# The closing LayerNorm of a fused decoder step: moments on ScalarE, gain and shift in three-operand steps on VectorE

## The reference, cut to what matters

```
def layer_norm(x, g, b):
    xf = x.astype(jnp.float32)
    mu = jnp.mean(xf, -1, keepdims=True)
    var = jnp.mean(jnp.square(xf - mu), -1, keepdims=True)
    y = (xf - mu) * lax.rsqrt(var + LN_EPS) * g.astype(jnp.float32) + b.astype(jnp.float32)
    return y.astype(x.dtype)
...
        f = moe_ffn(h, P['w_router'], P['router_bias'], P['ex_wg'][l], P['ex_wu'][l], P['ex_wd'][l])
        h = layer_norm(ALPHA * h + f, P['ln3_g'][l], P['ln3_b'][l])
```

## Time and profile before

| what | value |
|---|---|
| median of 3 runs | 1704.71 us (1702.11 to 1705.04) |
| the profiled execution's own time | 1703.08 us |
| its span in the trace | 1701.3 us |
| mean granted TensorE clock | 0.928 |
| busy: PE, PEld, DVE, ACT, POOL | 1481.7, 1062.2, 618.1, 499.7, 190.0 us |
| DMA traffic | 193.37 MB, mean 114 GB/s |

### The profile page before, as it was taken

How to read it: one execution, slowest core, us unless ns; L and a number is a source line. 1 busy time by engine, 2 the same in 40 slices (tenths; PEclk the granted TensorE clock), 3 DMA queues, 4 the chain that set the end, 5 groups by cost and what they waited for, 6 DMA issues and landing times. The chain is left out here.

```text
span 1701.3 us, 24683 instructions
## 1 busy us (share of the span) xinstructions
PE 1481.7 (87%) x9721; PEld 1062.2 (62%) x9722; DVE 618.1 (36%) x1005; ACT 499.7 (29%) x1050; POOL 190.0 (11%) x176
## 2 busy tenths in 40 slices
PE   4998999689999898889979989899459999999950
PEld 2445999545597677768869877687244544544420
DVE  3323462377512234447641033575421111111107
ACT  1124133278614434441222144312001111111114
POOL 0000000023200232200000000000001221222114
PEclk9998999789979799999989999999759999999985
DMA  8110121150013400012141164432625997843435
GB/s 311 56 56 20 44 55 38 36 174 26 1 50 102 136 15 2 3 56 109 44 136 38 50 255 167 147 106 87 247 111 189 329 313 238 252 89 85 97 51 227
DMA packets 85984, 193.37 MB, mean 114 GB/s; under 512 B 13204, under 2 KB 49179, under 8 KB 79475
## 3 DMA queue, kind: packets, MB, share of 16 engines
q1 hardware_dynamic: 76523, 157.14, 25.9%
q0 software_dynamic: 9216, 33.56, 8.5%
q10 hardware_dynamic: 144, 1.25, 0.2%
HBM read 148.50 MB, written 43.51 MB: 113 GB/s over the span
## 5 line engine op out<-in xcount | busy, mean ns | idle before, releaser
L3012 PE MATMUL bank<-arena,hT 128*128 x512 | 233.3, 599 | 2.2 <-DVE hT L3115 2.2
L3012 PEld LDWEIGHTS bank<-arena,hT 128*128 128x128 f32 x512 | 96.1, 193 | 111.3 <-issue 111.3
L3032 PE MATMUL bank<-arena,hT 128*128 x256 | 115.3, 593 | 0.7 <-ACT hT L3070 0.7
L473 PE MATMUL bank<-arena,hT 128*128 128x512 f32 x256 | 112.8, 599 | 0.0
L3110 DVE SCALAR_TENSOR_TENSOR hT<-bank,small,hT 128x256 f32<-128x256 f32 x32 | 15.5, 484 | 224.8 <-ACT hT L3076 224.8
L2134 PE MATMUL bank<-hT_rest,f_w_high 128*128 128x352 f32 x288 | 93.4, 324 | 0.0
L473 PEld LDWEIGHTS bank<-arena,hT 128*128 128x128 f32 x256 | 48.7, 193 | 58.3 <-issue 58.3
L2972 POOL DMA_INDIRECT expert_sums<-hT,row_slot x32 | 50.7, 1586 | 276.4 <-DVE hT L3121 173.0
L3032 PEld LDWEIGHTS bank<-arena,hT 128*128 128x128 f32 x256 | 46.3, 191 | 47.2 <-issue 47.2
L2963 POOL DMA_INDIRECT hT<-tokens,row_token x32 | 31.5, 984 | 317.5 <-POOLq L2740 288.3
L2133 PE MATMUL bank<-hT_high,q_w_high 128*128 128x352 f32 x192 | 62.4, 325 | 4.0 <-DVE q_w_low L2426 4.0
(11 more groups left out here) (470 smaller groups left out, 2963.7 us busy)
## 6 DMA issues: line engine op xcount, KB each, us to landing
arena<-in_ex_wg_dram SPq DMA_DIRECT2D x16, 1024.0 KB, 5.1
arena<-in_ex_wu_dram SPq DMA_DIRECT2D x16, 1024.0 KB, 8.9
arena<-in_ex_wd_dram SPq DMA_DIRECT2D x16, 1024.0 KB, 12.7
tokens<-h SPq DMA_DIRECT2D x24, 512.0 KB, 2.6
arena<-in_cache_mem_k_dram SPq DMA_DIRECT2D x8, 1024.0 KB, 4.9
arena<-in_w_in_dram SPq DMA_DIRECT2D x12, 512.0 KB, 4.1
h<-tokens SPq DMA_DIRECT2D x6, 1024.0 KB, 6.7
h<-in_x_prompt_dram SPq DMA_DIRECT2D x8, 512.0 KB, 8.8
```

Of the source, the lines that this page charges most:

```text
L473: last = nc.tensor.matmul(ps[bank][0:r, 0:n], hT[:, k, i * P:i * P + r], wt[:, k, col:col + n], start=(k == 0), stop=(k == KC - 1))
L3012: last = nc.tensor.matmul(ps[UPB[u % 2]][:, :], xT[:, u % 2, k, :], gate_up_of[:, bass.ds(slot, 1), :, k, :].rearrange("p a g f -> p (a g) ...
L3032: last = nc.tensor.matmul(ps[DNB[q]][:, :], hidT[:, u % 2, f, :], down_of[:, bass.ds(slot, 1), f, q * 512:(q + 1) * 512].rearrange("p a n ...
```

## The change

- **Loads of the two rows.** They leave the last stage. SP issues them in the experts, with `e == 0`, right behind the load of expert 3, into the last two of the nine tiles' places of `h` (`final_rows`), with a semaphore `c.fin_in` of their own.
- **Place of the data.** The nine tiles of `expert_sums` are loaded into `arena` (`z`) and stored from there.
- **Moments.** For tiles 0, 1 and 5 DVE still takes them, with the same three instructions. For tiles 2, 3, 4, 6, 7 and 8 ACT does: a pass `Identity` with a sum along the row (`accum_out`), that sum times -1/D (the shift), and a pass `Square` with the shift as bias and again a sum. The passes' full output goes to PSUM and is not read.
- **rstd.** ACT takes it for all nine tiles with the same two small instructions, from the variance or from the sum of squares scaled by 1/D.
- **Applying.** ACT's pass over the tile, DVE's multiply and GpSimd's add are gone. DVE does (x - mean)*g, or (x + shift)*g, in one `scalar_tensor_tensor`, then (x*rstd) + b in a second. GpSimd has no instruction in the last stage.

The core of the diff:

```
 stage_experts, SP:
                 if e == 0:
                     load_expert(c, sp, 3)
+                    for dst, name in zip(final_rows(c), ('ln3_g', 'ln3_b')):
+                        sp.dma_start(dst, row_bc(T[name][0])).then_inc(c.fin_in, 16)

+def final_rows(c):
+    flat = c.h.rearrange("p i d -> p (i d)")
+    return flat[:, 6 * D:7 * D], flat[:, 7 * D:8 * D]

 stage_combine, SP:
-                sp.dma_start(h[0:rows(i), i, :], c.sums_dram[i * P:i * P + rows(i), :]).then_inc(h_in[i], 16)
-                if i == 0:
-                    sp.dma_start(g, row_bc(T['ln3_g'][0])).then_inc(ln_in, 16)
-                    sp.dma_start(b, row_bc(T['ln3_b'][0])).then_inc(ln_in, 16)
+                sp.dma_start(z[0:rows(i), i, :], c.sums_dram[i * P:i * P + rows(i), :]).then_inc(z_in[i], 16)

 stage_combine, GpSimd:
-                gp.wait_ge(gained, i + 1)
-                nc.gpsimd.tensor_tensor(h[0:r, i, :], h[0:r, i, :], b[0:r, :], ALU.add).then_inc(normed, 1)

 stage_combine, DVE:
+            def affine(i):
+                dve.wait_ge(rstd_ok[i], 1)
+                if i in by_dve:
+                    dve.wait_ge(stats, by_dve.index(i) + 1)
+                    ins = nc.vector.scalar_tensor_tensor(x, x, mv[0:r, i, 0:1], g[0:r, :], ALU.subtract, ALU.mult)
+                else:
+                    ins = nc.vector.scalar_tensor_tensor(x, x, shift[0:r, i:i + 1], g[0:r, :], ALU.add, ALU.mult)
+                ins.then_inc(gained, 1)
+                dve.wait_ge(gained, i + 1)
+                nc.vector.scalar_tensor_tensor(x, x, rstd[0:r, i:i + 1], b[0:r, :], ALU.mult, ALU.add).then_inc(normed, 1)
+
+            moments(0)
+            moments(1)
+            dve.wait_ge(c.fin_in, 32)
             for i in range(TILES):
-                moments(i)
-                if i == 0:
-                    dve.wait_ge(ln_in, 32)
-                if i >= 1:
-                    gain(i - 1)
-            gain(TILES - 1)
+                affine(i)
+                if i + 2 in by_dve[2:]:
+                    moments(i + 2)

 stage_combine, ACT:
+            def root(i, x, scale):
+                link(nc.scalar.activation(rstd[0:r, i:i + 1], x, ACT.Ln, bias=c.eps3[0:r, :], scale=scale))
+                nc.scalar.activation(rstd[0:r, i:i + 1], rstd[0:r, i:i + 1], ACT.Exp, scale=-0.5).then_inc(rstd_ok[i], 1)
+
+            def of_act(i):
+                act.wait_ge(z_in[i], 16)
+                out = c.psum[0:r, 2 * (i % 2):2 * (i % 2) + 2, :].rearrange("p a n -> p (a n)")
+                link(nc.scalar.activation(out, z[0:r, i, :], ACT.Identity, accum_out=total[0:r, i:i + 1]))
+                link(nc.scalar.activation(shift[0:r, i:i + 1], total[0:r, i:i + 1], ACT.Copy, scale=-1.0 / D))
+                link(nc.scalar.activation(out, z[0:r, i, :], ACT.Square, bias=shift[0:r, i:i + 1], accum_out=square[0:r, i:i + 1]))
+                root(i, square[0:r, i:i + 1], 1.0 / D)
```

More of the change, by code:

```diff
@@ L2932, in stage_experts @@
     s = lambda n: c.sem(f"x{n}")
-    w_ok = s("wok")
+    w_ok, c.fin_in = s("wok"), s("fin")
     x_in = [s(f"x{u}") for u in range(2)]
@@ L3138, in _ @@
             finish(MOE_TILES - 1, U - 1, False)
+def final_rows(c):
+    flat = c.h.rearrange("p i d -> p (i d)")
+    return flat[:, 6 * D:7 * D], flat[:, 7 * D:8 * D]
 def stage_combine(c):
     nc, T, O = c.nc, c.T, c.O
-    c.place(start=0, cg=D, cb=D)
-    g, b = c.A("cg"), c.A("cb")
-    h = c.h
+    c.place(start=0, z=TILES * D)
+    z = c.A("z").rearrange("p (i d) -> p i d", i=TILES)
+    g, b = final_rows(c)
+    total, square, shift, rstd = (c.new_small(TILES) for _ in range(4))
+    mv = c.new_small(2 * TILES).rearrange("p (i n) -> p i n", n=2)
+    by_dve = (0, 1, 5)
+    by_act = [i for i in range(TILES) if i not in by_dve]
     s = lambda n: c.sem(f"c_{n}")
-    h_in = [s(f"h{n}") for n in range(TILES)]
-    ln_in, eps_ok, stats, scaled, gained, normed, stored, dve_chain, act_chain = (
-        s("ln"), s("eps"), s("stats"), s("scaled"), s("gained"), s("normed"), s("stored"), s("dve"), s("act"))
+    z_in = [s(f"z{n}") for n in range(TILES)]
+    eps_ok, stats, rstd_ok, gained, normed, stored, dve_chain, act_chain = (
+        s("eps"), s("stats"), [s(f"rstd{n}") for n in range(TILES)], s("gained"), s("normed"), s("stored"), s("dve"), s("act"))
     with nc.Block() as block:
@@ L3162, in _ @@
                 dst = O['y_prompt'][0, i * P:(i + 1) * P, :] if i < NT else O['y_sample'].rearrange("b t d -> (b t) d")
-                sp.dma_start(dst, h[0:rows(i), i, :]).then_inc(stored, 16)
+                sp.dma_start(dst, z[0:rows(i), i, :]).then_inc(stored, 16)
             sp.wait_ge(stored, 16 * TILES)
[L3166 to L3169, removed]
-                gp.wait_ge(gained, i + 1)
-                nc.gpsimd.tensor_tensor(h[0:r, i, :], h[0:r, i, :], b[0:r, :], ALU.add).then_inc(normed, 1)
         @block.vector
@@ L3178, in moments @@
             def moments(i):
[L3179 to L3184, removed]
-                r = rows(i)
-                dve.wait_ge(scaled, i + 1)
-                nc.vector.tensor_tensor(h[0:r, i, :], h[0:r, i, :], g[0:r, :], ALU.mult).then_inc(gained, 1)
-            for i in range(TILES):
-                moments(i)
-                if i == 0:
-                    dve.wait_ge(ln_in, 32)
-                if i >= 1:
-                    gain(i - 1)
-            gain(TILES - 1)
+                dve.wait_ge(z_in[i], 16)
+                ln_stats(nc, link, z, i, c.st[:, i % 2, :], mv[:, i, :]).then_inc(stats, 1)
+            def affine(i):
+                r = rows(i)
+                x = z[0:r, i, :]
+                dve.wait_ge(rstd_ok[i], 1)
[10 more added lines that the diff above has]
+            dve.wait_ge(c.fin_in, 32)
+            for i in range(TILES):
+                affine(i)
+                if i + 2 in by_dve[2:]:
+                    moments(i + 2)
         @block.scalar
@@ L3201, in _, with of_dve @@
             act.wait_ge(eps_ok, 1)
-            for i in range(TILES):
+            def root(i, x, scale):
                 r = rows(i)
[L3204 to L3209, removed]
+                link(nc.scalar.activation(rstd[0:r, i:i + 1], x, ACT.Ln, bias=c.eps3[0:r, :], scale=scale))
+                nc.scalar.activation(rstd[0:r, i:i + 1], rstd[0:r, i:i + 1], ACT.Exp, scale=-0.5).then_inc(rstd_ok[i], 1)
+            def of_dve(i):
+                act.wait_ge(stats, by_dve.index(i) + 1)
+                root(i, mv[0:rows(i), i, 1:2], 1.0)
+            def of_act(i):
+                r = rows(i)
+                act.wait_ge(z_in[i], 16)
[4 more added lines that the diff above has]
+                root(i, square[0:r, i:i + 1], 1.0 / D)
+            of_dve(0)
+            of_dve(1)
+            for i in range(2, TILES):
+                if i in by_dve:
+                    of_dve(i)
+                else:
+                    of_act(i)
 def build(nc, T, O):
```

## The result

The changed kernel takes **1694.16 us** in the median of 9 runs (1688.77 to 1699.05), the kernel before 1704.4 us in 9 runs beside it (1699.81 to 1709.98). The ratio is 0.9939, 95% interval 0.9919 to 0.9958. The profiled execution took 1695.61 us with a span of 1693.8 us.

What follows compares the result with a forecast made beforehand. TensorE bounds the whole; the edited last stage is bound by DVE and GpSimd in series. The new stage, laid out in time, ends 9.4 us earlier, giving 1693.7 to 1695.3, forecast 1694.5 us, range 1691.5 to 1698.5.

Steps and rivals of the forecast that it cites:

- GpSimd and DVE in series: Old last stage: DVE's gain reads only once GpSimd's add is over, without a semaphore; 3.5 us a tile.
- A pass of `scalar_tensor_tensor`, 1.31 us: DVE's new passes in the last stage: 1.31 us each, bounds 1.17 and 1.32, so 2.62 us a tile.
- ScalarE's tile, 3.5 us: ACT's sums and root for one tile in the last stage: 3.5 us, bounds 3.1 and 4.1 us.
- the 0.7 us that DVE was to wait for rstd(8): End of the last stage: DVE waits 0.7 us for ACT's last root and ends at 1689.5.
- Loads: Head of the last stage: without the rows in the queue, tile 1 lands at 1662.3 instead of 1665.87.
- The tail: The last store, from DVE's end to the span's end, takes 2.4 us as before.
- The sum: Stage ends at 1691.9, 9.4 us earlier: 1693.7 from the profiled execution, 1695.3 from the median, forecast 1694.5 us.
- A sign of being wrong: Whole execution: a span's end past 1693.5, against 1691.9 expected, makes the forecast wrong.
- The rows' loads at no cost: Experts: two row transfers behind expert 3's weights cost nothing, as SP's queue is served in order and expert 3's load covers them.
- the 2.5 us of an ordered queue: Experts: without expert 3's load as cover, the rows' 1.05 MB at 418 GB/s delay PE's start by 2.5 us.
- The rivals: ScalarE sets the pace, 1697.2 (0.10); rows delay first gather, 1697.0 (0.04); partial gain, about 1703 (0.03); stretched passes, 1709.6 (0.03).
- The stretched passes: Rival, last stage: DVE's eighteen passes run at 2.15 us each, stage 5.7 us later, 1709.6 us; chance 0.03.

Runs made afterwards that it cites:

- the two repetitions: The changed kernel traced twice more with nothing altered: last stage 32.67 and 32.78 us, ratios to the kernel before 0.9927 and 0.9941.
- the last version: Changed kernel with rows copied to PSUM, GpSimd taking second steps of tiles 1, 3, 5, stores ordered by readiness: stage 31.06 us, ratio 0.9919.

## Why the prediction was right, by its own steps

- **GpSimd and DVE in series.** Right, and now shown: with the adds on DVE the gains took 1.17 us, with a PSUM operand they took 1.17 us beside GpSimd's adds, and idle adds stretched four of the new kernel's passes to 3.4 us.
- **A pass of `scalar_tensor_tensor`, 1.31 us.** 1.28 us (1.23 to 1.28). The linked step was as I had it, 1.31 to 1.32; but the first step of a tile doesn't wait for the last of the tile before and starts 0.08 us ahead of its recorded end, so a tile takes 2.52 us and not 2.62. That is 0.9 us over nine tiles. The estimate of 1.13 us from the cycle counts in the errata section of "VectorE: DVE Perf Modes" in the Trainium skill is too low here too.
- **ScalarE's tile, 3.5 us.** 3.11 us, almost the lower bound. The pass into PSUM took 1.01 us, no more than one into SBUF; the pass with one pointer operand 1.12, where I had priced the one with two at 1.24; the small scaling 0.23 instead of 0.33; and the next tile's pass overlaps the end of the root, 0.43 instead of 0.57. So the 0.7 us that DVE was to wait for rstd(8) did not come: it waited for none, though with only 0.05 us to spare for rstd(8).
- **Loads.** Right: moments of tile 1 ended 6.3 us after the first load issue, as laid out (1663.8-1657.45 = 6.35).
- **The tail.** Right: 2.3 us against 2.4.
- **The sum.** The stage was to be 9.4 us shorter and is 11.1: 0.9 us from the tiles' passes and 0.7 us from ScalarE make up nearly all of the rest. On the runs 10.2 us were measured. That 1694.5 lies so near 1694.16 is luck: runs stray by 5 us to both sides, and the stage's gain was 1.7 us larger than forecast; the stage is the firm number.
- **A sign of being wrong came.** A span's end past 1693.5 was to make the forecast wrong, and the first trace ends at 1693.8. It came through the 3.6 us ahead of the stage, not through the stage, and the two repetitions end at 1691.4 and 1691.5. The sign was badly chosen: it left 1.6 us over the forecast end of the span, and the stages ahead stray by more than that. A bound on the stage alone would have told.
- **The rows' loads at no cost.** Right, but the reason given was half wrong. SP's transfers do land in order, and the rows landed behind the weights. But the gather doesn't stand in that queue: with the rows ahead of the weights the cost is 0.7 to 1.2 us in one trace, not the 2.5 us of an ordered queue.
- **The rivals.** None came. The stretched passes came in the one kernel where GpSimd read SBUF beside DVE steps with two SBUF tensors, at 3.4 us a pass. The rule of the Trainium skill that two SBUF sources which are not bf16 halve the rate ("Vector Engine (DVE) Microarchitecture Reference", points that are easy to get wrong) does not hold for these steps: 1.23 to 1.28 us for 1024 columns in all eighteen.

## What to carry to other kernels

When a two-source step of VectorE takes a time that isn't its own, look at what GpSimd reads in that moment: if the step ends a fixed time after GpSimd's, here 1.08 us, then for such steps the two engines are one engine, and work on the second is not hidden. One operand in PSUM separated them here. And once an engine is busy throughout, what stands ahead of and behind its work counts in full: two loads moved out of the head of a queue were worth 3.5 us, the order of the stores 1.3 us in the last version, and a pass takes 1.3 us.

## What the runs showed of the hardware that was not expected

- The exclusion holds in both directions, and the one recorded 0.05 us later can go first (the add at 1673.27 against the step at 1673.22, and so in three of the four pairs).
- GpSimd multiplying a 128x1024 tile by a per-partition scalar took 2.84 to 2.85 us, longer than its add of two tensors of that size, 2.35 us.
- Loads that spread one row of 4 KB over 128 partitions kept the DMA engines fully busy at 240 GB/s, expert weights at 414 GB/s. This is no fixed price of such loads: in the change, from 1275 to 1277.5, SP's queue moved 0.61 MB, the rows among it, in 59.5% of the engines' time, which is 410 GB/s of busy time. What made the difference is open.
- ScalarE writes 1024 columns to PSUM in 1.01 us, against 1.06 us into SBUF, there in another function.
- The gather of rows, issued by GpSimd, moved no packet in its first 4 us, in the kernel before, in the change and with the rows ahead of it alike.
